# Projections of a one-layer decoder step: weights loaded as half of the rows by 512 columns

## The reference

```
h = rms_norm(x)                          # x: 264 tokens x 2048
z = h @ w_in                             # 2048 x 13312: conv B,C,X | q | k | v | mq | gates
y_conv = (zb * conv3(zc * zx)) @ w_conv_out
y_diff = diff_attn(q, k, v) @ w_diff_out # 8 heads; the 8 samples see 16 pages x 128 cached keys
mk, mv = split(rms_norm(mem) @ w_mem_kv) # 256 memory tokens
y_mem  = mem_attn(mq, mk, mv) @ w_cross_out
x = x + (sum_b sigmoid(g_b) * y_b) @ w_o
x = x + peer_ffn(rms_norm(x))            # 16 of 16384 experts for each of 8 heads and token
```

## Time and profile before

| | us |
|---|---|
| median of 3 runs | 2757.74 (2751.84 to 2759.45) |
| profiled execution | 2753.93 |
| its span, first to last instruction | 2752.2 |
| PE busy | 2449.5 (89%) |
| DVE busy | 1433.6 (52%) |
| POOL busy | 1063.3 (39%) |
| ACT busy | 353.3 (13%) |

### The profile page before, as it was taken

One profiled execution on the slowest core, in us unless ns is written; L12 is line 12 of the kernel. 1 busy time (PEld: TensorE's weight loads), 2 busy tenths in 40 slices (PEclk: granted clock), 3 DMA queues, 4 the chain that ended last, 5 costly groups with the idle time before them and its releaser, 6 DMA issues.

```text
span 2752.2 us, 27802 instructions
## 1 busy us (share of the span) xinstructions
PE 2449.5 (89%) x9109; PEld 1570.1 (57%) x9109; DVE 1433.6 (52%) x2306; ACT 353.3 (13%) x781; POOL 1063.3 (39%) x953
## 2 busy tenths in 40 slices
PE   9999999989999999999997787776999597777777
PEld 7888887868766678888885233332434142233333
DVE  3465566962322223002478877884554656555543
ACT  2111000003222211001112101111011011111110
POOL 1265566020122200000056565654444564446542
PEclk9999999999999999999998999998989899999999
DMA  7698898594799965447498999999999999999998
GB/s 225 229 342 312 317 345 318 192 345 145 268 345 350 354 235 187 140 150 244 129 368 341 422 419 417 415 416 422 421 410 422 413 420 418 420 418 416 417 421 372
DMA packets 305904, 919.33 MB, mean 334 GB/s; under 512 B 15738, under 2 KB 196050, under 8 KB 236756
## 3 DMA queue, kind: packets, MB, share of 16 engines
q0 software_dynamic: 122448, 725.64, 65.5%
q1 hardware_dynamic: 183332, 192.20, 21.3%
HBM read 909.08 MB, written 8.72 MB: 333 GB/s over the span
## 4 chain that ended last, share of the span: by engine, by line
PE 31%; DMA 23%; DVE 15%; issue 14%; POOL 13%; POOLq 3%; ACT 1%; DVEq 0%; SPq 0%; ACTq 0%
DMA sb_bregion<-in_peer_u_dram,sb_ring 13%; PE ps L770 12%; PE ps L782 6%; PE ps L676 4%; DMA sb_mkv<-in_peer_u_dram,sb_ring 3%; POOL sb_ring L447 3%; DVE sb_bregion L1968 3%; DMA sb_S<-in_peer_u_dram,sb_ring 3%; POOL sb_mkv L447 3%; PE ps L1021 2%; PE ps L872 2%; POOL sb_bregion L548 2%; POOLq L438 2%; POOL sb_wring L548 2%; DVE sb_mkv L1968 1%
## 5 line engine op out<-in xcount | busy, mean ns | idle before, releaser
L1021 PE MATMUL ps<-sb_wring,sb_ring 128*128 128x512 f32 x992 | 456.9, 610 | 84.9 <-DMA sb_wring<-in_peer_v_dram,sb_ring 84.3
L676 PE MATMUL ps<-sb_hT,sb_wring 128*128 128x264 f32 x1792 | 409.4, 389 | 7.1 <-DMA sb_wring<-in_w_in_dram 7.1
L1968 DVE CUSTOM_DVE_ANT_0 sb_bregion<-sb_bregion,sb_rows 128x2048 f32<-128x2048 f32 x128 | 293.5, 2293 | 214.4 <-DMA sb_bregion<-in_peer_u_dram,sb_ring 207.2
L1021 PEld LDWEIGHTS ps<-sb_wring,sb_ring 128*128 128x128 f32 x992 | 186.1, 194 | 354.5 <-issue 260.6
L770 PE MATMUL ps<-sb_hT,sb_wring 128*128 128x264 f32 x1536 | 366.5, 389 | 13.9 <-ACTq L1173 10.6
L676 PEld LDWEIGHTS ps<-sb_hT,sb_wring 128*128 128x128 f32 x1792 | 340.3, 192 | 66.8 <-ACTq L1150 4.6
L770 PEld LDWEIGHTS ps<-sb_hT,sb_wring 128*128 128x128 f32 x1536 | 287.7, 190 | 77.7 <-issue 27.3
L1021 PE MATMUL ps<-sb_oreg,sb_ring 128*128 128x512 f32 x496 | 238.9, 632 | 72.8 <-DMA sb_oreg<-in_peer_v_dram,sb_ring 50.9
L1021 PE MATMUL ps<-sb_hT,sb_ring 128*128 128x512 f32 x496 | 231.6, 613 | 55.0 <-DMA sb_hT<-in_peer_v_dram,sb_ring 50.2
L548 POOL DMA_INDIRECT sb_bregion<-in_peer_u_dram,sb_ring x132 | 186.4, 1412 | 215.5 <-DVEq L1359 181.1
L1021 PEld LDWEIGHTS ps<-sb_oreg,sb_ring 128*128 128x128 f32 x496 | 97.1, 202 | 213.4 <-issue 147.2
(11 more groups left out here) (374 smaller groups left out, 2776.6 us busy)
## 6 DMA issues: line engine op xcount, KB each, us to landing
sb_wring<-in_w_in_dram SPq DMA_DIRECT2D x52, 2048.0 KB, 12.7
sb_ring<-in_cache_k_dram POOLq DMA_DIRECT2D x64, 512.0 KB, 7.0
sb_mkv<-in_cache_k_dram POOLq DMA_DIRECT2D x64, 512.0 KB, 6.7
sb_mkv<-in_cache_v_dram POOLq DMA_DIRECT2D x48, 512.0 KB, 7.1
sb_rows<-in_cache_v_dram POOLq DMA_DIRECT2D x47, 512.0 KB, 7.2
sb_wring<-in_w_mem_kv_dram SPq DMA_DIRECT2D x8, 2048.0 KB, 10.3
sb_wring<-in_w_o_dram SPq DMA_DIRECT2D x8, 2048.0 KB, 8.1
sb_S<-in_cache_v_dram POOLq DMA_DIRECT2D x22, 512.0 KB, 6.9
```

Of the source, the lines that this page charges most:

```text
L676: last = mm(ps[:, (2 * r + c) % 4, 0:NT], wring[:, r, k, c * P:(c + 1) * P], rhs[:, k, :], start=(k == 0), stop=(k == KC - 1))
L1021: last = mm(ps[:, 4 * t + q, :], diag[:, k % 4, :], e_slots[v % ER][:, q * 512:(q + 1) * 512], start=False, stop=q_stop, skip_group_check= ...
L1968: st(V.tensor_tensor_reduce(out=u_slots[n % UR], in0=u_slots[n % UR], in1=h2, scale=1.0, scalar=0.0, op0=ALU.mult, op1=ALU.add, accum_out= ...
```

## The change

The same two 2 MB buffers are read under another shape, `whalf`: buffer 0 holds the upper 1024 rows (k = 0 to 7) of 512 columns and buffer 1 the lower 1024 (k = 8 to 15). PE runs k = 0 to 7 of four chunks, in four banks, and then k = 8 to 15 of the same four. A load now has 512 contiguous columns in each row of the matrix (2 KB) in place of 256 (1 KB); its size stays. This holds for the projections by `linear` from w_in, and for the memory's keys and values, where a matmul now writes 512 columns and each piece is a whole bank: 8 pieces in place of 16. The gates, w_o and the expert queries keep blocks of 256 columns. A semaphore `half_full` tells SP when the first half has been used. The transposes of x for k = 14 and 15 move behind the first half chunk. The diff at its core:

```diff
+        whalf = wring[:, :, :, :].rearrange("p r (k two) n -> p r k (two n)", two=2)
...
-            def stream(n, src, col, c0, before):
...
+            def fetch_half(h, src, col):
+                sp.dma_start(whalf[:, h], src[:, h * BC:(h + 1) * BC, ds(col, 2 * BLK)]).then_inc(w_landed[h], 16)
+            def stream_halves(n, src, col, h0, c0, chunks):
+                if c0:
+                    sp.wait_ge(s["half_full"], h0)
+                fetch_half(0, src, col)
+                if c0:
+                    sp.wait_ge(s["chunk_full"], c0)
+                fetch_half(1, src, col)
+                with sp.Fori(0, n - 1) as i:
+                    sp.wait_ge(s["half_full"], i + (h0 + 1))
+                    fetch_half(0, src, i * (2 * BLK) + (col + 2 * BLK))
+                    sp.wait_ge(s["chunk_full"], i * chunks + (c0 + chunks))
+                    fetch_half(1, src, i * (2 * BLK) + (col + 2 * BLK))
...
-                    sp.wait_ge(s["chunk_full"], C_O - 2)
+                    sp.wait_ge(s["half_full"], H_GATE)
...
+            def half_chunk(h, c, rhs, fresh):
+                for k in range(h * BC, (h + 1) * BC):
+                    if fresh:
+                        pe.wait_ge(s["xT_scaled"], k + 1)
+                    last = mm(ps[:, c, 0:NT], whalf[:, h, k % BC, c * P:(c + 1) * P], rhs[:, k, :], start=(k == 0), stop=(k == KC - 1))
+                return last
...
+                    pe.wait_ge(w_landed[0], i * 16 + 16 * pair)
+                    for c in range(4):
+                        pe.wait_ge(s["chunk_taken"], i * 4 + (n0 + c + 1))
+                        if fresh and first:
+                            pe.wait_ge(s["xT_taken"], 8 + c)
+                        last = half_chunk(0, c, rhs, fresh and first and c == 0)
+                        if c == 3:
+                            last.then_inc(s["half_full"], 1)
+                        if c == 0:
+                            if first and pending:
+                                pending()
+                            elif turn and not first:
+                                turn(3, i * 4 + (n0 - c0 - 1))
+                    pe.wait_ge(w_landed[1], i * 16 + 16 * pair)
+                    for c in range(4):
+                        half_chunk(1, c, rhs, fresh and first and c == 0).then_inc(s["chunk_full"], 1)
+                        if aside:
+                            aside(n0 - c0 + c)
+                        if turn and c:
+                            turn(c - 1, i * 4 + (n0 - c0 + c - 1))
...
-            linear(G_QKV, 4, C_QKV, hT, turner(C_QKV, R_QKV), fresh=True, aside=after_query)()
+            linear(G_QKV, 4, C_QKV, hT, turner(C_QKV, R_QKV), pending=turn_last_columns, fresh=True, aside=after_query)()
...
-                        for k in range(KC):
-                            last = mm(ps[:, 2 * r + t, 0:BLK], memT[:, k, t * P:(t + 1) * P], wring[:, r, k, :], start=(k == 0), stop=(k == KC - 1))
...
+                            for k in range(h * BC, (h + 1) * BC):
+                                last = mm(ps[:, 2 * g + t, :], memT[:, k, t * P:(t + 1) * P], whalf[:, h, k % BC, :], start=(k == 0), stop=(k == KC - 1))
...
+            for n in range(8):
+                memory_chunk(n)
+                if n == 1:
+                    root(4, small[:, 3, 0:60])
+                if n == 3:
+                    root(5, small[:, 3, 0:8])
```

More of the change, by code:

```diff
@@ L229, in build @@
         G_QKV, G_CONV, G_MEM, G_GATE, G_O, G_PQ = 0, 16, 28, 36, 60, 68
-        C_QKV, C_CONV, C_MEM, C_O, C_PQ = 0, 32, 56, 72, 88
+        C_QKV, C_CONV, C_MEM, C_O, C_PQ = 0, 32, 56, 64, 80
+        H_CONV, H_MEM, H_GATE = 8, 14, 18
         R_QKV, R_O, R_PQ = 0, 32, 48
@@ L304, in fetch @@
                 sp.dma_start(wring[:, r], src[:, :, ds(col, BLK)]).then_inc(w_landed[r], 16)
-            def stream(n, src, col, c0, before):
[L308 to L319, removed]
+            def fetch_half(h, src, col):
[12 more added lines that the diff above has]
+                    fetch_half(1, src, i * (2 * BLK) + (col + 2 * BLK))
+            stream_halves(8, w_in, 3 * DC, 0, C_QKV, 4)
+            stream_halves(6, w_in, 0, H_CONV, C_CONV, 4)
+            stream_halves(4, w_mem, 0, H_MEM, C_MEM, 2)
             def gate_weights(b, n, r, i=0):
@@ L638, in _, with turn_columns @@
                 turn_x(2, k).then_inc(s["xT_full"], 1)
-            for k in range(7, KC):
+            def turn_columns(k):
                 pe.wait_ge(s["xT_taken"], k - 6 if k < 14 else k - 2)
@@ L643, in _, with turn_last_columns @@
                 turn_x(2, k).then_inc(s["xT_full"], 1)
+            def turn_last_columns():
+                turn_columns(14)
+                turn_columns(15)
+            for k in range(7, 14):
+                turn_columns(k)
                 if k == 7:
@@ L666, in turn_memory, with chunk @@
                 transpose_rows(h2_rows, k, 6 + k % 2, TILES[0:2]).then_inc(s["xT_full"], 1)
-            def chunk(r, c, n, rhs, fresh=False):
+            def chunk(r, c, n, rhs):
                 pe.wait_ge(s["chunk_taken"], n + 1)
-                if fresh:
-                    pe.wait_ge(s["xT_taken"], 11)
                 for k in range(KC):
+                    last = mm(ps[:, (2 * r + c) % 4, 0:NT], wring[:, r, k, c * P:(c + 1) * P], rhs[:, k, :], start=(k == 0), stop=(k == KC - 1))
+                last.then_inc(s["chunk_full"], 1)
@@ L1154, in _, with memory_chunk @@
             act.wait_ge(s["token_done"], 2 + TS)
-            def memory_chunk(i, q):
-                act.wait_ge(s["chunk_full"], i * 4 + (C_MEM + q + 1))
-                st(A_(mkv[:, q % 2, ds(i * (2 * BLK) + (q // 2) * BLK, BLK)], ps[:, q % 4, 0:BLK], ACT.Copy, scale=stat[:, 3 + q % 2:4 + q % 2]))
+            def memory_chunk(n):
+                g, t = n // 2, n % 2
+                act.wait_ge(s["chunk_full"], C_MEM + n + 1)
+                st(A_(mkv[:, t, g * 2 * BLK:(g + 1) * 2 * BLK], ps[:, n % 4, :], ACT.Copy, scale=stat[:, 3 + t:4 + t]))
                 act.sem_inc(s["chunk_taken"], 1)
[L1160 to L1167, removed]
+            for n in range(8):
[4 more added lines that the diff above has]
+                    root(5, small[:, 3, 0:8])
             def sigmoid(q):
@@ L1536, in memory_key_norm @@
             def memory_key_norm():
[L1538 removed]
+                dve.wait_ge(s["chunk_taken"], C_MEM + 4 + 4)
                 sqm = cflat[:, 2 * BC * NT:2 * BC * NT + D].rearrange("p (t n) -> p t n", t=2)
```

21 lines of the change are left out of this document (12 added, 9 removed).

## The result

| kernel | median of its runs, us | lowest to highest | runs |
|---|---|---|---|
| before | 2755.81 | 2747.83 to 2759.45 | 8 |
| changed | 2762.66 | 2760.57 to 2764.11 | 8 |

The ratio is 1.0027, with a 95% interval from 1.0018 to 1.0036. The change costs 6.85 us. That is under the 0.3% that I had called the bound of what can be told, but the interval leaves out 1: the kernel is slower, where I had forecast 2.8 us less. The profiled execution of the changed kernel has a span of 2761.1 us against 2752.2, so 8.9 us have to be found in its trace.

A forecast was written before the change was run, and what follows sets the result against it. The prediction took POOL and DVE as the bound until about 607 us, then PE's gate chunks. Its terms, -0.8 at the start and -2 for memory scores, summed to -2.8 us: 2755 us from a 2757.74 median, range 2746 to 2765.

The forecast's parts named there:

- What bounds the kernel: Up to about 607 us the late track is POOL and DVE, with PE 10.58 us early; afterwards PE's gate chunks.
- my signs for being right: Sigmoid ended by DVE at 602 to 607, PE waiting about 22 us, 10.80 us groups, queries sent at 105.
- my signs for being wrong: Groups over 10.8 us, DVE waiting for cache pages, PE waiting for w_in near 39 us, or PE releasing a sigmoid.
- the memory's scores: DVE's 9.4 us of waits for cached memory keys before the meeting: -2 us, bounds -5 and +3.
- Bunched chunks: Projections: four chunks finish 3.6 us apart, then none for 14.3; last query chunk no later, so 0 us.
- Fewer waits for weights: PE between 100 and 470 us: at most 10.1 us of weight waits go, giving 0 at the end.
- The memory's pieces: PE's 4.22 us wait at 486.16 goes, wide matmuls cost up to 2.4 us more; 0 at the end.
- The start: First projection matmuls begin about 1.6 us sooner, so PE's clock may rise sooner: -0.8 us, between 0 and -1.6.
- The second half of the weights: Load landing at 38.8 us, on time by 0.4 us: 0, each microsecond of later landing costing one.
- The page loop: POOL's groups of four pages stay at 10.80 us: 0, between 3 us less and 3 us more for its stalls.
- The rivals of a gain: PE's gain reaches the end, 2745 us, chance 0.08; quieter DMA shortens stalls and memory waits, 2742 us, chance 0.09.
- After 607: Behind the meeting, work, banks, buffers and queues are unchanged: 0 us.

The follow-up runs named there:

- root_early: Changed kernel with ACT taking the queries' square root ahead of its wait for the first key chunk; 2751.89 us, ratio 0.9986.
- before_root_late: Kernel before the change with the queries' square root behind the second key chunk, not the first; 2762.57 us, ratio 1.0033.
- narrow_memory: root_early with the memory's keys and values back in blocks of 256 columns; 2751.61 us, ratio 0.9987.
- all_turned_first: root_early with all of x's transposes ahead of the first half chunk again; 2752.27 us, ratio 0.9986.
- after_root_later: Changed kernel with the queries' square root behind the second key chunk, not the first; 2765.46 us, ratio 1.0034.
- root_early_warm: root_early plus 8 unused matmuls of constants on PE while it waits for the first sigmoid; 2750.76 us, ratio 0.9980.
- warm11: root_early plus 11 unused matmuls of constants on PE while it waits for the first sigmoid; 2749.98 us, ratio 0.9984.

## Why the prediction was wrong

**What bounds the kernel** was right. The first sigmoid is still ended by DVE, and PE's share of busy time meant nothing: it has 9.2 us less to do in a kernel that is slower. Of my signs for being right, two failed, the queries at 105 us (116.19) and the sigmoid at 602 to 607 (613.41); none of my signs for being wrong came, because none of them looked at what stands behind the chunk in ACT's queue. That 2762.66 lies in my range of 2746 to 2765 is luck. The range's upper end adds 3 us of POOL's stalls, 3 of the memory's scores and 2 that belong to no term of mine; the first two did not come, and the delay that did come stands in no bound.

***Bunched chunks*: this step failed.** I wrote what is queued behind a finished chunk as "ACT's copy, PE's turn and the copy to rows", and took 0 because the last query chunk is finished no later. That chunk is indeed on time (84.85 against 85.22). But the chunk whose finish moved is the next one, the first key chunk, and in ACT's queue the queries' root stands behind it. I looked at `root(4)` and `root(5)` under the memory's pieces, and not at `root(3)`. The term is +10.31 at the queries in place of 0 (+10.67 of DVE's wait), and root_early and before_root_late show it from both sides. The rows to see it were within reach: five half chunks of 3.58 us are 17.9 until the first key chunk, and ACT's rows of the kernel before at 92.99 and 93.48 show the root's table load right behind that chunk's copy.

**Fewer waits for weights** was right: 3.0 and 0.9 us are left of 7.1 and 3.0, and nothing of it reaches the end. The waits between 100 and 470 us (who, for what, us in total, times, longest):

```profile
POOL sb_mkv L448 <- issue: 66.5, 55, 10.1
...
PE ps L696 <- DMA sb_wring<-in_w_in_dram: 3.0, 2, 2.1
...
PE ps L790 <- DMA sb_wring<-in_w_mem_kv_dram: 0.9, 1, 0.9
```

**The memory's pieces:** the wait of 4.22 us went, as said. The 256 wide rows are busy 110.3 us, not 115.6 to 118.0: both bounds were too high. PE has its last work ahead of the meeting done at 584.08 (602.54 less 18.46), 12.6 us sooner than 596.72 (607.30 less 10.58; I had said 11.9), and waits 18.46 + 10.97 = 29.4 us rather than 22, since the meeting itself is late. narrow_memory shows that none of it counts.

**The start:** -0.8 was said; -0.37 was read in the changed kernel, and 0.60 between root_early and all_turned_first. Both are smaller than the 1.02 us by which two kernels with the same start differ at the query's last transposes (84.11 in after_root_later, 85.13 in root_early_warm), so neither the size nor the sign is shown. The Trainium skill's rule of the prediction ("TensorE: Matmul & The Clock Gate", What's actually happening), that the clock follows how busy PE has been lately, agrees with the meeting: the clock is 0.50 from 603 to 609 in root_early, where PE had waited 12.03 us, and 1.00 in warm11, where it had worked. The windows at 25 us lean the same way and do not decide it.

**The second half of the weights** was safe. The first two loads land after 11.9 and 30.0 us, in place of 13.2 and 34.4. The margin is as thin as I said: in narrow_memory, with the same start, the second lands after 34.0 us and PE waits 1.4 us for it at 38.5.

```profile
DMA to landing us min/median/max: 11.9/21.0/30.0
```

**The page loop** was right: 132.58 to 143.38 is again 10.80 us. (These are the first and second groups; before the change the first began at 121.69 and the second at 132.52.) The pages did not come late: their median is 6.6 us (6.7 in the earlier trace rows), the maximum 9.3 (8.9). With equal turns my estimate from the rows was 8.0 us. The Trainium skill ("DMA: Bandwidth & Descriptors", Queues, rings and completion order), by whose packets of several descriptors I had given the weights a bigger turn, stood beside that estimate; the measurement decides against that use of it.

**The rivals of a gain** did not come either. PE did not set the meeting. The weights do load the engines less, but POOL's stalls at the turn of its loop stay at 10.1 us at the longest (9.91 in the earlier trace rows); what they hang on is still open.

**The memory's scores:** -2 was said and -2.8 came, but not for my reason. PE is as far ahead in root_early, and there DVE waits 9.6 us; it waits 8.9 to 9.9 in the other kernels with the early root, 9.1 in before_root_late and 6.4 in after_root_later. The short waits are in the two kernels that have both the halves and a late root, so neither alone makes them. What does was not tried and stays open; one guess is how these loads fall against SP's.

**After 607:** I said 0. In the changed kernel the 16 rows take 5.39 us in place of 4.15, and that is +1.24 us to DVE's multiply. warm11, which fills PE's wait ahead of them, gets 3.73 us, so a wait of PE has a price at the meeting. That a longer wait has a higher one is not shown. The same rows take 4.15, 4.50 and 4.85 us in the three kernels with the old blocks, where PE waits 9.85 to 10.58 us, and 4.40 and 5.07 in all_turned_first and root_early, where it waits 28.0 us in both, with one transpose in between. So part or all of the 1.24 can be the difference between one execution and the next.

The sum, term by term, to DVE's multiply behind the meeting: -0.4 at the start, +10.7 root, -2.8 memory scores, +1.2 in the rows behind the meeting, and -0.8 that I did not place, make the +7.9 read there. Only the root's term is shown by runs to be the change's own. The +1.0 from there to the span is open too; it is less than the 3.5 us between the changed kernel's fastest and slowest run.

## What to carry to other kernels

When a change moves the moment at which something is finished, go through every engine's queue that waits for that moment, and read what stands behind the wait, related or not: a small request of the critical track behind an unrelated wait costs all of the wait. Put such requests ahead of waits for bulk work; here that move alone took 10.8 us off the changed kernel. And an engine that is early may not be ready at full speed: in root_early PE's clock stood at 0.50 from 603 to 609 us, after its wait, and the 8 matmuls behind the attention's transposes took 5.07 us, against 3.73 in warm11. In this kernel that reached DVE's next multiply; that it reached the end is not shown.

## What I had not expected of the hardware

Between 120 and 470 us the queue of the weights, before:

```profile
q1 hardware_dynamic: 48995, 49.80, 43.2%
```

and after:

```profile
q1 hardware_dynamic: 24527, 49.45, 38.7%
```

The columns are packets, MB and the share of 16 engines' time. Over 350 us that is 48.6 engine-microseconds for each MB with rows of 1 KB, and 43.8 with rows of 2 KB: 10% less, with the median landing of a load down from 14.1 to 12.0 us. It repeats: 48.5 and 49.0 in before_root_early and before_root_late, and 44.0, 43.7 and 44.4 in root_early, after_root_later and all_turned_first. The share counts the time that packets took beside the cache pages, so it is not what a row costs alone. The longer rows do what they promise; this kernel had little use for it.

The clock of PE fell again soon after it was idle: in root_early_warm the 9.60 us of matmuls from 591.39 brought it to 1.00 from 597 to 603 (0.54 from 591 to 597), and with a gap of 3.20 us behind them it averaged 0.53 from 603 to 609.
